# First items of a product operand tile by operand tile, and a split of queries and keys without a staging buffer

## The reference

```python
# block 1, layer 0: HGRN2 mixer;  layer 1: q from x, k, v and a forget gate from kv_w, softmax attention
mix = hgrn2_mixer(hn, ...)                       # layer 0
mix = fox_mixer(hn, b_w_q, b_w_out, k_sh, v_sh, c_sh)   # layer 1
    logits = (q @ k.T) / 8 + (c_i - c_j); p = softmax(mask(logits)); o = p @ v   # 16 heads of 64
h = h + rmsnorm(mix, g[1])
h = h + rmsnorm(conv_ffn(rmsnorm(h, g[2])), g[3])       # up, causal conv of 3 taps, silu(gate) * value, down

# block 2, layer 0: gated delta rule;  layer 1: latent attention (MLA)
mod = silu(c) @ ada_w[layer] + ada_b[layer]      # shift, scale, gate for mixer and ffn: 6 x 1024 columns
h = rmsnorm(x, g) * (1 + scale_m) + shift_m
x = x + gate_m * mixer(h)
x = x + gate_f * swiglu(rmsnorm(x, g') * (1 + scale_f) + shift_f)
out = rmsnorm(x, final_g)
```

## Time and profile before

| | us |
|---|---|
| time, median of 3 runs (1595.53 to 1597.49) | 1596.88 |
| the profiled execution's own time | 1595.38 |
| its span, first to last instruction | 1593.6 |
| TensorE busy | 1469.6 |
| VectorE busy | 1041.1 |
| ScalarE busy | 779.9 |
| GpSimd busy | 281.6 |
| mean granted TensorE clock | 0.967 of full |

### The profile page before, as it was taken

How to read it: one execution, slowest core, us unless ns; L and a number is a source line. 1 busy time by engine, 2 the same in 40 slices (tenths; PEclk the granted TensorE clock), 3 DMA queues, 4 the chain that set the end, 5 groups by cost and what they waited for, 6 DMA issues and landing times. The chain is left out here.

```text
span 1593.6 us, 29023 instructions
## 1 busy us (share of the span) xinstructions
PE 1469.6 (92%) x11301; PEld 1404.5 (88%) x11301; DVE 1041.1 (65%) x1727; ACT 779.9 (49%) x1272; POOL 281.6 (18%) x384
## 2 busy tenths in 40 slices
PE   5999879999788898999998899989999989999997
PEld 4999769999686667999997789989999987899997
DVE  5664678877765447788757755357787665677643
ACT  5655644454454444555545555564443555534341
POOL 0000101220053330121100153102332100132110
PEclk8999999999998899999998999999999998999999
DMA  6432535659431224465771311236765733275451
GB/s 275 176 126 106 192 122 193 233 188 335 177 139 74 80 104 162 166 234 211 255 252 58 132 54 54 68 121 222 277 248 208 242 106 137 99 291 185 145 181 44
DMA packets 41141, 265.80 MB, mean 167 GB/s; under 512 B 4561, under 2 KB 5713, under 8 KB 15441
## 3 DMA queue, kind: packets, MB, share of 16 engines
q1 hardware_dynamic: 41040, 264.44, 46.0%
HBM read 263.38 MB, written 1.05 MB: 166 GB/s over the span
## 5 line engine op out<-in xcount | busy, mean ns | idle before, releaser
L224 DVE TENSOR_TENSOR w_lo<-raw,w_hi 128x2048 fp32r<-128x2048 f32 (+2 forms) x207 | 425.4, 2059 | 238.4 <-ACT w_hi L220 234.7
L220 ACT ACTIVATE w_hi<-raw 128x2048 fp32r<-128x2048 f32 (+3 forms) x224 | 385.8, 1727 | 38.1 <-PE bank L398 34.0
L396 PE MATMUL bank<-z_hi,w_hi 128*128 128x258 f32 x752 | 215.4, 286 | 5.1 <-DVEq L931 4.2
L397 PE MATMUL bank<-z_lo,w_hi 128*128 128x258 f32 x752 | 213.0, 283 | 0.0
L398 PE MATMUL bank<-z_hi,w_lo 128*128 128x258 f32 x752 | 212.3, 282 | 0.0
L396 PE MATMUL bank<-x_hi_up,w_hi 128*128 128x272 f32 (+1 forms) x704 | 203.5, 289 | 8.2 <-DVE x_lo_up L688 8.1
L398 PE MATMUL bank<-x_hi_up,w_lo 128*128 128x272 f32 (+1 forms) x704 | 201.7, 287 | 0.0
L397 PE MATMUL bank<-x_lo_up,w_hi 128*128 128x272 f32 (+1 forms) x704 | 201.4, 286 | 0.0
L396 PEld LDWEIGHTS bank<-z_hi,w_hi 128*128 128x128 f32 x752 | 142.1, 189 | 6.7 <-DVE w_lo L224 3.0
L397 PEld LDWEIGHTS bank<-z_lo,w_hi 128*128 128x128 f32 x752 | 143.2, 190 | 0.1
L398 PEld LDWEIGHTS bank<-z_hi,w_lo 128*128 128x128 f32 x752 | 142.4, 189 | 0.0
(11 more groups left out here) (450 smaller groups left out, 3832.1 us busy)
## 6 DMA issues: line engine op xcount, KB each, us to landing
raw<-w_up SPq DMA_DIRECT2D x44, 1024.0 KB, 4.8
raw<-w_gu SPq DMA_DIRECT2D x44, 1024.0 KB, 4.8
work<-w_ada SPq DMA_DIRECT2D x27, 1024.0 KB, 4.9
raw<-w_down SPq DMA_DIRECT2D x32, 704.0 KB, 4.3
raw<-w_dn SPq DMA_DIRECT2D x32, 704.0 KB, 4.1
raw<-w_a_in SPq DMA_DIRECT2D x16, 1024.0 KB, 5.5
mod_w_down<-w_ada SPq DMA_DIRECT2D x12, 1024.0 KB, 6.2
raw<-w_gdn_qkv SPq DMA_DIRECT2D x12, 1024.0 KB, 4.8
```

Source lines behind the costliest of these rows:

```text
L220: act.activation(w_hi[:, s, 0:blocks * P], raw[:, s, 0:blocks * P], ACT.Copy).then_inc(hi_split.sem, 1)
L224: dve.tensor_tensor(w_lo[:, s, 0:blocks * P], raw[:, s, 0:blocks * P], w_hi[:, s, 0:blocks * P].bitcast(F32), ALU.subtract).then_inc(lo_sp ...
L396: pe.matmul(o, w_hi[:, s, b], x_hi[:, xk, cols[0]:cols[1]], start=begin, stop=False)
L397: pe.matmul(o, w_hi[:, s, b], x_lo[:, xk, cols[0]:cols[1]], start=False, stop=False)
```

## The change

Four things are changed.

1. `hosting`: with a distance of two or more, the host items are the second, fourth (or second, sixth, ...) item in place of the first, third.
2. `Product.tensor`: with an entry or `x_ready` and without halves, the first two items (`joint` = 2; one, if the product has a `root`) are issued k tile by k tile over all their tiles and banks. The root's sum then comes after both tiles of the first item. Mla_out, with neither entry nor `x_ready`, and the second products of the feed-forwards keep their order. The first mixer does the same for its first item, Fox for its first four query tiles (in banks 0, 1, 4, 5), Gdn for its first three tiles (gate inputs, keys 0 and 1).
3. Fox: ScalarE and VectorE write the high and low parts of queries and keys straight to their places in `heads`, `keys_hi` and `keys_lo`, in two instructions of 64 partitions each. GpSimd copies only the other 64 partitions of the keys: 4 copies for a key tile, none for a query tile. `fox_high` and `fox_low` are gone.
4. Fox and Gdn raise `item_out` for the product after them (all their items at once) ahead of the last head, and ahead of the first split of the output, instead of at their end.

```diff
                 def hosting(r, s):
                     if limited:
-                        return isinstance(r, int) and r - first < hosts * every and (r - first) % every == 0
-                    return (s - first) % SLOTS % every == 0
+                        return isinstance(r, int) and r - first < hosts * every and (r - first) % every == min(1, every - 1)
+                    return (s - first) % SLOTS % every == min(1, every - 1)
...
+                joint = 0 if halves or not (entry or x_ready) else 1 if root else 2
+
                 def tensor(pe):
+                    def joint_items():
+                        for r in range(first + 1, first + joint):
+                            pe.wait_ge(lo_split.sem, r + 1)
+                            pe.wait_ge(item_out.sem, r - 1)
+                        for k in range(k_tiles):
+                            if entry:
+                                pe.wait_ge(entry.split.sem, entry.split.at(k + 1))
+                            if x_ready:
+                                pe.wait_ge(x_ready.sem, x_ready.at(x_step * (k // x_pair + 1) + x_off))
+                            for r in range(first, first + joint):
+                                s = r % SLOTS
+                                for t in range(tiles):
+                                    o = where(r, s, t)[:, 0:width]
...
+                                if k == k_tiles - 1:
+                                    last.then_inc(item_done.sem, 1)
...
-                        for t in range(tiles):
+                        if isinstance(r, int) and r - first < joint:
+                            if r == first:
+                                joint_items()
+                            if root and r == first:
+                                root.pe_root(pe)
+                        for t in range(0 if isinstance(r, int) and r - first < joint else tiles):
...
         class Fox:
...
                 def bank_of(event):
-                    return bank[turn[event] % 2]
+                    m = turn[event]
+                    return bank[(0, 1, 4, 5)[m]] if m < 4 else bank[m % 2]
...
-                        if m >= 2:
-                            tile_taken(pe, in_turn[m - 2])
+                        if m >= 4:
+                            tile_taken(pe, in_turn[m - 2 if m >= 6 else m - 4])
...
+                def halves_of(event):
+                    n = index_of(event)
+                    if part_of(event) == "q":
+                        return [(slice(0, dv), heads[0:dv, n, 0, :], heads[dv:P, n, 0, :]),
+                                (slice(dv, P), heads[dv:P, n, 1, :], heads[0:dv, n, 1, :])]
+                    hi, lo = keys_hi[:, n % 3, :, :], keys_lo[:, n % 3, :, :]
+                    return [(slice(0, dv), hi[0:dv, 0, :], lo[0:dv, 0, :]), (slice(dv, P), hi[dv:P, 1, :], lo[dv:P, 1, :])]
...
-                            pe.wait_ge(stacked.sem, stacked.at(4 * KD + 8 * t + 8))
+                            pe.wait_ge(stacked.sem, stacked.at(4 * t + 4))
...
+                            dve.wait_ge(made_high.sem, made_high.at(split_at[event] + 1))
+                            for rows, hi, lo in halves_of(event):
+                                if part_of(event) == "q":
+                                    last = dve.scalar_tensor_tensor(lo, o[rows, :], 0.125, hi.bitcast(F32), ALU.mult,
+                                                                    ALU.subtract)
+                                else:
+                                    last = dve.tensor_tensor(lo, o[rows, :], hi.bitcast(F32), ALU.subtract)
                             last.then_inc(made_low.sem, 1)
...
+                            if part_of(event) == "k" and index_of(event) >= 3:
+                                act.wait_ge(scored.sem, scored.at(2 * (index_of(event) - 2)))
+                            for rows, hi, _ in halves_of(event):
+                                last = act.activation(hi, bank_of(event)[rows, 0:T1], ACT.Copy,
+                                                      scale=0.125 if part_of(event) == "q" else 1.0)
+                            last.then_inc(made_high.sem, 1)
...
+                            for i, part in enumerate((keys_hi, keys_lo)):
+                                for a in range(2):
+                                    mine, twin = (slice(dv * a, dv * a + dv), slice(dv - dv * a, P - dv * a))
+                                    pool.tensor_copy(part[twin, t % 3, a, :],
+                                                     part[mine, t % 3, a, :].bitcast(F32)).then_inc(stacked.sem, 1)
...
+                            if n == n_heads + 1:
+                                act.wait_ge(copied_out.sem, copied_out.at(len(copies)))
+                                act.wait_ge(made_low.sem, made_low.at(len(split_at)))
+                                act.sem_inc(item_out.sem, len(names))
...
         class Gdn:
...
+                    def first_items():
+                        for r in (first, first + 1):
+                            pe.wait_ge(lo_split.sem, r + 1)
+                        for k_ in range(KD):
+                            pe.wait_ge(entry.split.sem, entry.split.at(k_ + 1))
+                            for i, (r, t, done) in enumerate(((first, 0, item_done), (first + 1, 0, half_done),
+                                                              (first + 1, 1, item_done))):
```

## The result

The changed kernel takes 1605.19 us (median of 8 runs), the kernel before 1595.05 us in the runs beside it. The ratio is 1.0069, with an interval of 1.0052 to 1.0085. I had forecast 1590.3 us, faster. The profiled execution has a span of 1602.0 us, 8.4 more than the 1593.6 of before. The page: busy time of each engine, and the granted clock in tenths for 40 slices.

The account below looks back on a forecast made before the run. TensorE, 92% busy, was taken as the bound, so only its idle time or half-clock stretches could pay. Stage terms summed to −6.55 us from 1595.38, giving 1588.8, with the median 1.5 above: 1590.3 us; range 1583 to 1600.

Parts of the forecast that it names:

- Fox, "So a wait such as the 1.86 us ... shrinks by 1.93 − 0.83 = 1.1: −3.2": Fox's three TensorE waits for key copies: 1.93 us of copies dropped, 0.83 added per key tile; −3.2 us in all.
- Fox, the query phase "0": Fox's query tiles: first four end 1.1 us earlier, but the seventh waits for VectorE, given 0.44 more per tile; 0.
- Fox, first head "−0.8": Fox's first head, 5.49 us late at 485.56: −1.1 from fewer copies, +0.3 from the weight split; −0.8 us.
- the prediction's own sign of being wrong, after 485: Fox's first head after 485 would show that the pairs cost more than the copies they replace.
- Fox, "I take half, −2.5": Half-clock stretches behind two Fox gaps, three of 1.65 us each: half the gain taken, −2.5 us.
- Rival C: Full clock kept in Fox (−2.5 more) and after 853, mixer costs nothing, up0/up1 regain 0.7: median 1585 us; chance 0.20.
- Delta-rule mixer, "+2.1": Three joint tiles delay the gate inputs, partly hidden by the gates' chain: +2.1 us, bounds 0 and +4.7.
- B_out, "+0.6": Joint first items in b_out: likewise as a_out, a readout stall of 0.8 against 0.2 won; +0.6 us.
- the readout's stall in up0 and up1: Item 2 waits for item 0's banks: 2.6 us readout, 0.87 us cover, so a 1.75 us stall.
- gu1 in sum: In gu1, the late-column gap goes (−2.9), half clock behind it goes (−1.65), joint item wins 0.45: −5.0 us.
- dn0: Its host shifts by 1 to 2.4 us against about 2 us of slack: +0.2 us (0 to +0.7).
- Rival A: Joint items' stalls without wins cost 11.4 us, hosts bring 5.8, Fox 2: net +3.6, 1600.5 us; chance 0.12.

Follow-up runs that it names:

- e4: Kernel before plus only Fox's in-place split of queries and keys and the earlier signal, query tiles not joint: 1600.17 us, ratio 1.0032.
- e8: Kernel before plus Fox's in-place split and earlier signal, with VectorE's weight split moved behind the next head's step, query tiles not joint: 1584.97 us, ratio 0.9943.
- e5: Kernel before plus only Fox's four first query tiles joint: 1599.09 us, ratio 1.0030.
- e6: Kernel before plus only the delta-rule mixer's three joint tiles and its earlier signal: 1601.98 us, ratio 1.0053.
- e3: Kernel before plus only the shifted host items: 1591.39 us, ratio 0.9985.
- e1: Changed kernel with the whole Fox part put back as in the kernel before: 1603.31 us, ratio 1.0058 to the kernel before.

## Why the prediction was wrong

**Fox, "So a wait such as the 1.86 us ... shrinks by 1.93 − 0.83 = 1.1: −3.2"** failed. The size of the shrink was about right (0.95 to 0.98), and so was the full time for 64 partitions: ACT 0.39 and VectorE 0.44 us for each half, as for a whole tile before (0.39 and 0.44): halving the partitions saved nothing. Wrong was that TensorE's waiting ends with this wait. The next one, 0.16 us for the probabilities at 521.07, shows that a second chain was due just then, and it runs over the very engines that the edit loads. Each shrink so cost 0.67 us net: e4 shows it, and e8 shows the chain.

**Fox, the query phase "0"** failed. I counted VectorE's 0.44 us per tile and took the wait at 460.27 to absorb the joint tiles. The joint tiles cost 3.2 us by themselves (e5) and the pairs 1.5 (e4); together they cost 2.4.

**Fox, first head "−0.8"**: from the gate turn to the head it was −1.8 (3.99 instead of 5.79 us), but the gate turn came 6.2 us later, 4.2 of them lost inside Fox. So the first head stands at 489.99, and the prediction's own sign of being wrong, after 485, was met. In e4 the head comes only 0.25 us later in Fox than before, so the pairs alone hardly delay it, and the rest came with the joint query tiles.

**Fox, "I take half, −2.5"** failed: Fox up to b_out has 32.3 us at half clock instead of 27.3. In e8, with the waits gone, no half clock is left from head 2 on. Rival C was right about Fox in such a kernel, and not about this one.

**Delta-rule mixer, "+2.1"** was mis-sized: +3.2 alone, +4.3 in the changed kernel, up to the tokens. The first key tile is taken at 874.6, 2.8 us later in the mixer than before, inside the 2.1 to 3.65 that I had worked out. But the stall at the squares that I had put at 1 us, and only for the upper bound, is 4.2: VectorE reads the gate inputs at 868.41, 10.2 us after the start instead of 6.4, and the key tile stands behind the gates' chain on ACT and VectorE. The 2.7 us behind the tokens are slow clock (6.8 us of it, none before), for which the sum had nothing.

**B_out, "+0.6"** was mis-sized too: +1.6, of which 1.2 us are idle time.

**Right**: the readout's stall in up0 and up1 (1.73 and 1.70; forecast 1.75), down1, gu0's and gu1's gap and the full clock behind it, gu1 in sum (−5.2; forecast −5.0). **dn0** was mis-sized (+2.7, forecast +0.2): its slack of 2 us was used up by a load that is issued at the end of a chain, not by VectorE.

**Rival A** had the sign and most of the places of the stalls (+3.6), but not the price of Fox. The range ended at 1600, since I had bounded Fox at −2, where it was +4.9: from the waits that the edit shortens, without a bound for the work that it adds to a chain.

## What to carry to other kernels

When an edit shortens a wait, look at the next instructions on the waiting engine and read how long their operands had been ready: no more than that can be gained. If one of them waits too, as here, nothing is gained, and if the edit loads its chain it is a loss. Tiles that are filled together are read out together: the first one's readout loses the cover that the others gave. Order the long operation that nobody waits for (here a weight split of 2.3 us) behind the short ones that open two chains, before making those shorter.

## What the runs showed of the hardware

In Fox slow clock came with the holes. From head 6 on e4, with waits of 1.8 us, had 17.1 us at half clock, the kernel before 10.2, and e8, whose waits are about 0.75 us, none. From Fox's first matmul to b_out's e8 has 9.3 us less idle time than e4 and is 15.6 us shorter: between these two a wait cost 1.7 times its length. But the holes alone don't settle it: behind the gate tokens of the delta-rule mixer the idle time is 9.6 to 10.0 us in every kernel, and 0 to 9.7 us are at half clock. The same stage with the same instructions moved by up to 2.8 us between kernels that did not touch it (Fox 154.9, 155.0, 156.6 and 157.7 us in the kernel before, e6, e3 and e1), with idle time up to b_out that differs by 0.2 us at most: a stage compared in one profile has this uncertainty, and the waits in it are what can be compared closely. An operation over 64 partitions cost on ACT and VectorE what one over 128 had cost in the kernel before (0.39 and 0.44 us for 272 columns in either case, read from PSUM).
